# A gated DeltaNet block, one head after the other, rewritten as a pipeline over heads

## What is computed

```python
proj = h @ lp["w_in"]                       # q, k, v, z_g of a head: 128 columns each
qkv = jax.nn.silu(_dwconv_centred(qkv, conv_w, conv_b))   # 5 taps
q = _l2norm(q) * (GDN_DK ** -0.5);  k = _l2norm(k)
gc = jnp.cumsum(g, axis=-1)
decay = jnp.exp(jnp.where(incl, gc[..., :, None] - gc[..., None, :], -jnp.inf))
lmat = jnp.where(strict, jnp.einsum("bhnik,bhnjk->bhnij", kb, k) * decay, 0.0)
tinv = triangular_solve(eye + lmat, eye)    # one 128 x 128 inverse for a tile and a direction here
attn = jnp.einsum("bhnik,bhnjk->bhnij", q, k) * decay
def step(S, xs):                            # the chain over tiles, forward and backward
    v_new = u_c - w_c @ S
    o = qg_c @ S + attn_c @ v_new
    S = S * glast_c + kdec_c.T @ v_new
    return S, o
o = _rms(o_f + _flip(o_b)) * gdn_norm_w * jax.nn.silu(z_g)
```

## Time and profile before

| | us |
|---|---|
| median of 3 runs (2470.24 to 2475.63) | 2472.2 |
| the profiled execution | 2473.93 |
| its span, first to last instruction | 2472.1 |
| of it the DeltaNet stage, 684.0 to 1603.3 | 919.3 |
| one head of it, from one scaling row L948 (1154.49) to the next (1267.14) | 112.65 |

### The profile page before, as it was taken

The page is one execution under the profiler, slowest core; times in us unless marked ns, Lnnn a source line. Parts: engine busy times, 40 slices in busy tenths (PEclk is TensorE's granted clock), DMA queues, the critical chain, the costliest instruction groups (busy, mean ns, idle before and its releaser), DMA issues. The chain is left out here.

```text
span 2472.1 us, 26913 instructions
## 1 busy us (share of the span) xinstructions
PE 2175.3 (88%) x10146; PEld 1351.8 (55%) x10146; DVE 1016.1 (41%) x1968; ACT 526.1 (21%) x1227; POOL 274.7 (11%) x325
## 2 busy tenths in 40 slices
PE   3899999999879898989888898799999886699886
PEld 2455645555447585766757585655555444444332
DVE  3456555564634535445354545300000047422224
ACT  1323313232123232333323232300000000011111
POOL 0020100202010201202020201100000000221112
PEclk9999999999889898989899998999999997799998
DMA  8121201211010101010101101098342183499973
GB/s 283 49 60 43 52 17 35 60 43 43 0 49 4 36 2 36 4 34 4 34 5 36 36 2 28 13 323 215 100 130 77 37 314 154 150 382 420 398 322 132
DMA packets 173598, 257.31 MB, mean 104 GB/s; under 512 B 14695, under 2 KB 142504, under 8 KB 159184
## 3 DMA queue, kind: packets, MB, share of 16 engines
q1 hardware_dynamic: 146936, 216.95, 25.4%
q10 hardware_dynamic: 18488, 23.54, 3.3%
q0 software_dynamic: 8096, 15.75, 1.8%
HBM read 229.68 MB, written 39.10 MB: 109 GB/s over the span
## 5 line engine op out<-in xcount | busy, mean ns | idle before, releaser
L664 PE MATMUL bank<-hT,shared 128*128 128x512 f32 x512 | 253.0, 630 | 12.9 <-DMA negm<-in_levels_dram 8.1
L1156 PE MATMUL bank<-hT,shared 128*128 128x512 f32 x384 | 169.3, 594 | 2.6 <-DVE xT L1529 1.8
L2128 PE MATMUL bank<-ring,xgT 128*64 128x512 f32 (+1 forms) x416 | 149.1, 628 | 17.6 <-DMA ring<-in_w_exp_up_dram 12.2
L1010 DVE TENSOR_TENSOR conv<-bank,negm 128x512 f32<-128x512 f32 x144 | 82.3, 599 | 184.5 <-PE bank L677 184.5
L1211 PE MATMUL bank<-wz,hT 128*128 128x512 f32 x320 | 153.4, 618 | 0.0
L664 PEld LDWEIGHTS bank<-hT,shared 128*128 128x128 f32 x512 | 94.9, 201 | 96.2 <-issue 87.9
L677 PE MATMUL bank<-D_,MT 128*128 128x128 f32 x960 | 125.5, 280 | 0.0
L1710 DVE SCALAR_TENSOR_TENSOR prod<-gth,bank 128x512 f32<-128x512 f32 x16 | 11.0, 688 | 272.7 <-PE bank L1680 272.7
L685 PE MATMUL bank<-DT,conv 128*128 128x128 f32 x960 | 121.6, 276 | 0.0
L1156 PEld LDWEIGHTS bank<-hT,shared 128*128 128x128 f32 x384 | 71.3, 191 | 84.1 <-issue 84.0
L677 PEld LDWEIGHTS bank<-D_,MT 128*128 128x128 f32 x960 | 114.0, 192 | 2.8
(11 more groups left out here) (413 smaller groups left out, 3410.8 us busy)
## 6 DMA issues: line engine op xcount, KB each, us to landing
shared<-in_w_in_dram SPq DMA_DIRECT2D x58, 512.0 KB, 6.5
ring<-in_w_exp_gate_dram SPq DMA_DIRECT2D x26, 1024.0 KB, 11.8
ring<-in_w_exp_up_dram SPq DMA_DIRECT2D x26, 1024.0 KB, 19.1
ring<-in_w_exp_down_dram SPq DMA_DIRECT2D x26, 1024.0 KB, 14.7
aw<-in_w_ada_dram SPq DMA_DIRECT2D x8, 2048.0 KB, 10.9
yd<-mzero ACTq DMA_DIRECT2D x1, 16128.0 KB, 107.5
aw<-in_w_ada_dram SPq DMA_DIRECT2D x8, 1024.0 KB, 21.1
wz<-in_w_in_dram SPq DMA_DIRECT2D x4, 2048.0 KB, 7.9
```

Of the source, the lines that this page charges most:

```text
L664: last = pe.matmul(bank[a][:, :], w4[:, n, k, :], hT[:, k, SEQ:T], start=(k == 0), stop=(k == KD - 1), skip_group_check=True)
L1010: TT(out=X[:, u0:u0 + n, :], in0=bank[XB[g]][:, 0:n * P].rearrange("p (u n) -> p u n", n=P), in1=m, op=ALU.mult).then_inc(s["g_Xkept"], 1)
L1156: pe.matmul(bank[a][:, :], wn(n)[:, k, :], hT[:, k, SEQ:T], start=(k == 0), stop=(k == KD - 1))
L2128: last = pe.matmul(bank[2 + slot][at, :], xgT[:, slot, k, at], wgu[w][:, k, :, :], start=(k == 0), stop=(k == KD - 1))
```

## The change

Only `deltanet` changes. The loop over heads becomes a software pipeline: each engine's program is now `inverse(h)` followed by `chain(h)`, and both carry work of head h + 1. Head 0's projections and preparation stand in front as a prologue, the last head has no next head in it, and the hardware loop holds two heads in one turn (buffers with a parity: `cur`, `neg`, `ber`, `kq`, `kn`, `vt`, `att`, `rn`).

- PSUM: the inverse keeps banks 0 to 4 only. A transpose now goes to the bank that its group's `blocks_X` uses (`xdv`), and group 2 has both halves of bank 4: its `blocks_DT` no longer adds into PSUM; VectorE adds the identity to X instead (one more 256-column instruction a level, L1190 of the new file). Banks 5, 6 and 7 serve projections, transposes and the chain.
- TensorE: `between` puts the projections of head h + 1 for k, q and v into levels 0, 1 and 2, the own head's z into level 3, the transpose of the last head's output into level 0, and turn k, the sums, turn kn and turn v into levels 3 to 5. The first two pieces of k stand ahead of the inverse. The products of k and q for head h + 1 and the segment sums stand at the start of the chain. The chain has no projection in it any more.
- VectorE: convolution, silu, sums, gate and kn of head h + 1 stand between the masks of levels 1 to 4; `strict`, `keep_M`, `first_blocks` and `add_one` (the old L985, L992, L996, L999) of head h + 1 stand inside the chain. The attention mask and the last head's normalisation and gating stand in level 0.
- ScalarE: evacuation, tanh and squares of head h + 1 between the copies of the levels; `vd` of the chain moves here from VectorE. `decay` and `keep_att` stand in chain steps 0 and 1.
- GpSimd: the masks `gm` and `bm` are written into the storage of `MT` and `D_`, after the last `blocks_X` of the inverse.
- The last state update of each chain (step 4), which no one read, is left out.
- SyncE loads the weights of head h + 2 for k, q and v during head h, and all four tiles of head 0 again at the start of the stage, `negm` after them.

The core of the diff:

```diff
-        XB = (0, 3, 6)
-        DTB = (1, 4, 7)
-        DB = (2, 5, 6)
-        dtv = lambda g, n: bank[DTB[g]][:, 0:n * P]
-        dv = lambda g, n: bank[DB[g]][:, 256 * (g == 2):256 * (g == 2) + n * P]
-
-        CHAIN = [(0, 0)] + [(1 + s, 4 - s) for s in range(4)]
...
+        dtv = lambda g: (bank[0][:, :], bank[2][:, :], bank[4][:, 0:256])[g]
+        xdv = lambda g: (bank[1][:, :], bank[3][:, :], bank[4][:, 256:512])[g]
...
+        LATB = (5, 6, 5, 6)
...
+        KSB, VNEWB, SUB, QSB, OB = two(6, 0), two(6, 1), two(5, 0), two(5, 1), two(7, 0)
...
+                def between(h, par, l, i, first, more):
+
+                    n = h + 1
+                    if l == 0:
+                        if more and i < 2:
+                            proj(n, K, 2 + i)
+                        if i == 2 and not first:
+                            turn_o(h - 1)
+                        if more and i == 4:
+                            pe.wait_ge(s["g_v"], h + 1)
+                            if not first:
+                                pe.wait_ge(s["g_head"], h)
+                            proj(n, K, 4)
+                    if l == 1 and more:
+                        if i == 0:
+                            pe.wait_ge(s["g_v"], h + 1)
+                            if not first:
+                                pe.wait_ge(s["g_head"], h)
+                        if i == 4:
+                            pe.wait_ge(s["g_raw"], 3 * n + 1)
+                        proj(n, Q, i)
+                    if l == 2 and more:
+                        if i == 0 or i == 4:
+                            pe.wait_ge(s["g_raw"], 3 * n + 1 + i // 4)
+                        proj(n, V, i)
+                    if l == 3:
+                        if more and i == 4:
+                            turn_k(n)
+                        if not first:
+                            if more and (i == 0 or i == 4):
+                                pe.wait_ge(s["g_raw"], 3 * n + 2 + i // 4)
+                            if not more and i == 0:
+                                pe.wait_ge(s["g_head"], h)
+                            proj(h, Z, i)
+                    if l == 4 and more and i == 1:
+                        sums(n, h)
+                    if l == 5 and more and i == 0:
+                        turn_kn(n, 1 - par)
+                    if l == 5 and more and i == 2:
+                        turn_v(n, h)
+
+                def inverse(h, par, first=False, more=True):
+                    fill = lambda l, i: between(h, par, l, i, first, more)
+                    if more:
+                        if first:
+                            pe.wait_ge(s["g_knT"], 1)
+                        else:
+                            pe.wait_ge(s["g_qs"], 4 * h)
+                        proj(h + 1, K, 0)
+                        proj(h + 1, K, 1)
...
+                        inner = l < LEVELS - 1
                         blocks_DT(h, l, 0)
+                        fill(l, 0)
                         blocks_DT(h, l, 1)
-                        if l < LEVELS - 1:
+                        fill(l, 1)
+                        if inner:
                             turn_D(h, 0, l)
                         blocks_DT(h, l, 2)
-                        if l < LEVELS - 1:
+                        fill(l, 2)
+                        if inner:
...
+                            fill(l, 3)
...
+                            fill(l, 4)
+
+                def chain(h, par, more=True):
+                    n = h + 1
+                    if more:
+                        products(n, 1 - par, 0)
+                        products(n, 1 - par, 1)
+                        pe.wait_ge(s["g_v"], n + 1)
+                    else:
+                        pe.wait_ge(s["g_zg"], h + 1)
+                    pe.wait_ge(s["g_DTkept"], 18 * h + 17)
...
+                        pe.wait_ge(s["g_R"], 5 * h + p + 1)
+                        for d, t in enumerate(tiles):
+                            last = pe.matmul(VNEWB[d], DT[:, unit(d, t), :], R[:, d, :], start=True, stop=True, skip_group_check=True)
+                        last.then_inc(s["g_vnew"], 1)
+                        if p == 0:
                             pe.wait_ge(s["g_DTkept"], 18 * h + 18)
                             if more:
-                                pe.wait_ge(s["gw_in"], 64 * h + 64)
-
-                        if more and p < 4:
-                            proj(0, [2 * p])
-                        pe.wait_ge(s["g_R"], 5 * h + p + 1)
...
-                        if more and p < 4:
-                            proj(0, [2 * p + 1])
...
-                        if more and p < 4:
-                            proj(0, [KD + 2 * p, KD + 2 * p + 1])
+                                products(n, 1 - par, 2)
+                                segments(n)
+                        if p < 4:
+                            pe.wait_ge(s["g_vd"], 4 * h + p + 1)
...
-                    if more:
-                        proj(1, range(KD - 1))
-                    pe.wait_ge(s["g_on"], h + 1)
-                    for t in range(NT):
-                        last = pe.transpose(bank[5 if t < 4 else 3][:, t % 4 * P:t % 4 * P + P], on[:, t, :], C(C_ID))
-                    last.then_inc(s["g_oturn"], 1)
-                    if more:
-                        pe.wait_ge(s["g_qs"], 4 * h + 4)
-                        proj(1, range(KD - 1, 2 * KD))
...
+                with pe.Fori(1, GH - 2, 2) as h:
+                    for a in range(2):
+                        inverse(h + a, 1 - a)
+                        chain(h + a, 1 - a)
...
+                        keep_D(h, g, g)
+                    if not first:
+                        squares_o(h - 1)
                     for l in range(LEVELS):
-                        keep_DT(l, 0)
-                        keep_DT(l, 1)
+                        if more and 1 <= l <= 3:
+                            raw(n, l - 1)
+                        if l == 4 and not first:
+                            tanh_z(h)
+                        if more and 2 <= l <= 4:
+                            tanh(n, l - 2)
+                        keep_DT(h, l, 0)
+                        keep_DT(h, l, 1)
...
+                                last = act.activation(vd[:, d, :], VNEWB[d], ACT.Copy, scale=ber[:, par, t, d:d + 1])
+                            last.then_inc(s["g_vd"], 1)
                         if p > 0:
                             act.wait_ge(s["g_O"], 5 * h + p)
                         for d, t in enumerate(tiles):
-                            last = act.activation(vn[:, d, :], bank[2][:, d * P:(d + 1) * P], ACT.Copy, scale=cur[:, 4, t, d:d + 1])
...
+                def chain(h, par, more=True):
+                    if more:
+                        roots(h + 1, 1 - par)
+                        pool.wait_ge(s["g_X"], 18 * h + 18)
+                        masks(h + 1, 1 - par)
                     for p in range(1, 5):
...
+
+                def strict(n, d):
+                    if d == 0:
+                        dve.wait_ge(s["g_dec"], n + 1)
+                        dve.wait_ge(s["g_bm"], 3 * n + 2)
+                    st.add(TT(out=di[:, d, :, :], in0=dec[:, d, :, :], in1=di[:, d, :, :], op=ALU.mult))
+
...
+                def inverse(h, par, first=False, more=True):
+                    n = h + 1
                     for l in range(LEVELS):
-                        for g, (u0, n) in enumerate(GROUPS):
-                            dve.wait_ge(s["g_X"], 18 * h + 3 * l + g + 1)
-                            m = negm[:, l, g:g + 1, :].broadcast_to([P, n, P]) if g < 2 else negm[:, l, :, :]
-                            TT(out=X[:, u0:u0 + n, :], in0=bank[XB[g]][:, 0:n * P].rearrange("p (u n) -> p u n", n=P), in1=m, op=ALU.mult).then_inc(s["g_Xkept"], 1)
+                        mask_X(h, l)
+                        if l == 0:
+                            mask_att(h, par)
+                            if not first:
+                                normed(h - 1)
+                            if more:
+                                begin(n, 1 - par)
+                            if not first:
+                                gated(h - 1)
+                        if more and 2 <= l <= 4:
+                            silu(n, 1 - par, l - 2)
+                        if more and 1 <= l <= 3:
+                            convolve(n, l - 1)
+                        if l == 4:
+                            if more:
+                                keep_sums(n)
+                            if not first:
+                                gate(h)
+                            if more:
+                                keep_kn(n, 1 - par)
+
```

714 lines of the change are left out of this document (431 added, 283 removed).

## The result

| | before | changed |
|---|---|---|
| median, us (4 runs each) | 2471.8 (2470.24 to 2475.63) | 2402.2 (2399.45 to 2403.51) |
| profiled execution, us | 2473.9 | 2399.45 |
| its span, us | 2472.1 | 2397.6 |
| first projection to the start of `merge`, us | 914.4 | 840.8 |

The ratio is 0.9711 with a 95% interval of 0.9699 to 0.9723: the changed kernel is 2.9% faster. The forecast was 2398 in a range of 2366 to 2456.

What follows compares the result with a forecast made beforehand. TensorE was taken to bound the stage: 91 us of products, 13 waiting, 8 slow clock a head. Heads of 101.9 instead of 112.8 us and the ends gave 73.6 us less, 2398 against the runs, range 2366 to 2456.

Steps and rivals of the forecast that it cites:

- Seven heads and the ends: Whole DeltaNet stage: first identity product at 748.3, head 0 96.8, six heads 611.4, last with end 73.2; stage end 1529.7 us.
- Inverse and levels: TensorE's inverse: 35.7 us a head, 14.2 a level with projection; masks on time, 5.18 us wait for VectorE's identity block gone.
- The 1.1 us for levels 4 and 5: End of the inverse: level 5's masks 0.6 us late, and 0.5 for kn's evacuation ahead of `turn_v`.
- The chain: Bare chain of each head, 25.1 us: 1.8 + 1.9 for products and segments, 2.3 for VectorE's lateness, 19.1 for the steps.
- The lock with GpSimd, 0.8: Level 5: GpSimd's masks hold VectorE's new identity addition, both inputs in SBUF, by up to one mask; 0.8 us a head.
- No gap in it is longer than about 2 us, so I count no slow clock.: One full head of 101.9 us against 112.8: TensorE's gaps stay short, so no time was charged for slow clock.
- The prologue: Before head 0's inverse: negm's wait goes, weights are loaded again, first identity product about 2.5 us later, at 748.3.
- The last head: Last head: 35.7 + 8.65 + 0.56 + 19.1 = 64.0 us, then the stage's end as before, 9.2 us.
- rival 1: The clock falls in the bare chain: about 8 us a head, 56 in seven, total 2454; chance 0.13.
- Rival 2: The chain's new VectorE and ScalarE work shows in full: 4 to 6 us a head, total about 2433; chance 0.14.
- Rival 3: Woven queues hold each other in the inverse's levels: 6.8 us for each of 21 levels, total 2541; chance 0.06.
- Rival 4: TensorE was full after all, its idle and slow time comes back somewhere: total 2472; chance 0.05.

Runs made afterwards that it cites:

- the second kernel: Changed kernel with the loop kept for heads 1 to 4 and the next k projection's first two pieces issued ahead of the jump: 2388.2 us, ratio 0.9659.
- kernels 5 and 6: Changed kernel, TensorE's heads written out, four k products in the chain: 2395.3 us; the same plus both `strict` early and att's masks in the chain: 2366.6 us.
- the unwoven kernel: Changed kernel with the projections of q, v and z in one piece at their level's end: 2412.4 us, ratio 0.9749.
- kernels 3 and 8: Changed kernel with both `strict` moved behind R of step 1: 2397.2 us; the same with TensorE's heads also written out: 2384.8 us.
- kernel 10: Changed kernel with TensorE's heads written out, `strict` early and the 20 sums split into two pieces of ten: 2380.8 us, ratio 0.9619.

## Why the prediction was right, step by step

- **Seven heads and the ends.** Forecast from the first product to `merge`: 1529.7 - 688.9 = 840.8 us. Measured: 840.79. That is luck in part, since four terms are off and cancel: the prologue (59.4 forecast, 62.8 measured) by +3.4, head 0 by -1.9, six heads (611.4, 606.6) by -4.8, the last head with the end (73.2, 76.4) by +3.2. Of the -4.8, 3.4 us are a slip of the sum: head 6 has no next k to begin, and I charged it a full head.
- **Inverse and levels.** A level with a projection was said to take 14.2 to 14.3 and takes 14.2, without a wait. The 5.18 us wait was said to go, and did, in all heads but the prologue. The 1.1 us for levels 4 and 5 are 0.43 for X and 0.84 for kn.
- **The chain.** Forecast 25.1, measured 23.2 (1116.67 to 1139.88, undisturbed head of the second kernel). Step 2 is late by 0.95 instead of 1.5, steps 3 and 4 not at all instead of 0.8, and the segments hide better. Its price was named rightly, cover that is lost, and kernels 5 and 6 show the size: products that are put back into the chain cost nothing there.
- **The lock with GpSimd, 0.8.** VectorE is held (L1190 takes 1.50 us beside the masks and 0.42 in the last head, which has none), but nobody waits for it:

```profile
1119.46 2.48 POOL L1060 TENSOR_TENSOR MT<-cst,cur 128x640 f32<-128x640 f32 x2 [1.73 <-PE bank L735]
1120.72 1.50 DVE L1190 TENSOR_TENSOR X<-X,cst 128x256 f32<-128x256 f32 x1
1122.14 2.50 DVE L1247 COPY small<-vt 128x128 f32<-128x128 f32 x2
1123.83 0.74 PE L681 MATMUL bank<-cst,shared 128*128 128x128 f32 x5 [0.84 <-ACT kq L930]
```

- **"No gap in it is longer than about 2 us, so I count no slow clock."** This is the step that failed. Two gaps of 3.05 us and their slow products cost 2 x 5.2 us, and none of my steps or rivals had them: I read what each engine runs and not where its program jumps. Slow stretches in heads 0, 3, 5 and 6 cost another 0.8 to 1.9 us each. A head without either is 99.2, not 101.9. The mean of the full heads, 1 to 5, is 101.9 all the same, as forecast, and that is luck: 2.7 us a head that were charged and did not come, against 2.7 of jumps and slow stretches that no step had.
- **The prologue.** negm's wait went, but the first product waits 7.88 us for the weights' transfer in its place. Normalised k (3.74) stands open there with nothing woven under it, and the identity blocks still show 3.94 with 3.6 us of head 1's k ahead of them:

```profile
PE bank L672 <- DMA shared<-in_w_in_dram: 7.9, 1, 7.9
PE bank L809 <- DVE DT L1179: 3.9, 1, 3.9
PE bank L681 <- DVE shared L1153: 3.7, 1, 3.7
```

- **The last head.** I took its level 0 as free. Without k's pieces in it, `turn_o` waits for VectorE:

```profile
1465.40 0.77 PE L681 MATMUL bank<-cst,gboth 128*128 128x128 f32 x5 [2.81 <-DVE gboth L1203]
```

- **Rivals.** The clock does fall in the bare chain, but for some 3 us at a time in three chains (heads 0, 3 and 5) and not throughout: rival 1 has its mechanism and, at about 0.9 us each, a twentieth of its price of 56 us (which was added wrongly: 5.4 and 3.5 are 8.9 a head, 62 in seven). The rule of the Trainium skill that stood behind it (page "TensorE: Matmul & The Clock Gate", section "A second HAM failure mode: psum-queue depth-cycling") agrees with that much. Rival 2 ends at 0.95 us a head. Rival 3 is excluded by the levels, in the unwoven kernel too. Rival 4 is wrong by the windows: 37 us of idle time went.

## What to carry to other kernels

Weaving one unit's preparation under the products of another pays where TensorE's record is busy but its clock is low: count the waits and the slow products behind them, then ask of each piece that is moved which gap it leaves bare (here the chain, whose places can be filled again at no cost). Look at a program's jumps as at any other step: a loop body that was doubled here started to load its code, and its jump cost nothing only with 3.4 us of products queued ahead of it, or with no loop at all. A late engine that nobody waits for becomes the next limit as soon as the work beside it is moved (the masks of att), so move both at once.

## What the runs showed of the hardware that was not expected

- A jump of the two-head loop: 3.05 us idle with a transfer of code in it, nothing with 3.4 us of products queued ahead; in the one-head loop no transfer of code at all. That the loading is what TensorE waits for is not shown by itself.
- Twenty one-column products in one row (2.29 us) were followed by some 3 us at the low clock in six heads of six (kernels 3 and 8); in two rows of ten, in two of six (kernel 10). In the changed kernel the one row did it in two heads of six, so what runs before it counts too.
- A plain copy from SBUF to SBUF on VectorE, 128x128, is held by GpSimd's masks as well: 2.50 us for two (L1247 above) and 0.35 for the same two without them. The Trainium skill, page "SBUF — State Buffer", section "Who interferes with whom", counts copies among the operations that can take the shared pair of ports, and the rows agree; the prediction gave the rule without its exception for such copies.

```profile
1501.27 0.35 DVE L1247 COPY small<-vt 128x128 f32<-128x128 f32 x2
```
